# Row sums of squares as two fp32r products, the second half a unit later

## The reference

```python
def rmsnorm(x, g):
    xf = x.astype(jnp.float32)
    y = xf * lax.rsqrt(jnp.mean(xf * xf, axis=-1, keepdims=True) + EPS)
    return (y * g).astype(x.dtype)

for l in range(DEPTH):                      # first_block
    if l < N_A:  x = x + short_conv_mixer(rmsnorm(x, attn_norm[l]), ...)
    else:        # k, v, c from rmsnorm(x, kv_norm); q, gate from rmsnorm(x, attn_norm[l])
        c = jnp.cumsum(jax.nn.log_sigmoid(f_logit), axis=1)
        ...
        x = x + o @ b_w_out[j]
    x = x + conv_ffn(rmsnorm(x, ffn_norm[l]), ...)
# second_block
h = _rms_norm(x, norm_mix_g[l]);  proj = h @ w_in[l]
...
x = x + merged @ w_out[l]
x = x + (jax.nn.silu(ff_gate) * ff_up) @ w_ffn_out[l]
```

## Time and profile before

| what | value |
|---|---|
| median of 3 runs | 2110.87 us (2110.78 to 2111.08) |
| the profiled execution, its own time | 2110.74 us |
| its span in the profile | 2108.9 us |
| PE busy | 2081.9 us, 99% |
| POOL busy | 1498.7 us, 71% |
| DVE busy | 927.7 us, 44% |
| ACT busy | 475.0 us, 23% |
| granted clock of TensorE | 1.00 |
| share of PE in the chain that ended last | 93% |

### The profile page before, as it was taken

The page is one execution under the profiler, slowest core; times in us unless marked ns, Lnnn a source line. Parts: engine busy times, 40 slices in busy tenths (PEclk is TensorE's granted clock), DMA queues, the critical chain, the costliest instruction groups (busy, mean ns, idle before and its releaser), DMA issues.

```text
span 2108.9 us, 29655 instructions
## 1 busy us (share of the span) xinstructions
PE 2081.9 (99%) x10652; PEld 1755.5 (83%) x10652; DVE 927.7 (44%) x1406; ACT 475.0 (23%) x977; POOL 1498.7 (71%) x1607
## 2 busy tenths in 40 slices
PE   7999999999999999999999999999999999999999
PEld 6888888888798887888888889989877888888887
DVE  6655655521445555655541166436643243222100
ACT  2002111100345554211100053231343112111000
POOL 6788888868854456888877766546545787777675
PEclk9999999999999999999999999999999999999999
DMA  4333333223432232333323333223322333333232
GB/s 153 94 110 103 99 99 91 86 84 101 116 92 81 81 91 75 99 91 99 99 72 96 102 87 85 65 71 81 83 68 70 90 100 93 96 99 99 73 93 85
DMA packets 368007, 192.65 MB, mean 91 GB/s; under 512 B 8640, under 2 KB 364320, under 8 KB 367920
## 3 DMA queue, kind: packets, MB, share of 16 engines
q1 hardware_dynamic: 364672, 186.28, 30.8%
q10 hardware_dynamic: 3248, 5.20, 0.8%
HBM read 189.32 MB, written 2.13 MB: 91 GB/s over the span
## 4 chain that ended last, share of the span: by engine, by line
PE 93%; DVE 4%; ACT 3%; issue 1%; ACTq 0%; DMA 0%; DVEq 0%
PE PS L519 22%; PE PS L521 22%; PE PS L520 22%; PE PS L801 2%; PE PS L803 2%; PE PS L802 2%; PE PS L817 2%; PE PS L819 2%; PE PS L818 2%; PE PS L684 2%; PE PS L686 2%; PE PS L685 2%; PE PS L999 1%; PE PS L1018 1%; PE PS L629 1%
## 5 line engine op out<-in xcount | busy, mean ns | idle before, releaser
L502 POOL TENSOR_TENSOR RING<-RAW,RING 128x512 fp32r<-128x512 f32 x704 | 966.9, 1373 | 58.7
L499 POOL TENSOR_SCALAR RING<-RAW 128x512 fp32r<-128x512 f32 x704 | 514.0, 730 | 376.2 <-PE PS L686 99.1
L519 PE MATMUL PS<-XH,RING 128*128 128x512 f32 x1336 | 522.2, 391 | 3.7 <-DVE XT L2232 2.5
L521 PE MATMUL PS<-XH,RING 128*128 128x512 f32 x1336 | 519.8, 389 | 0.0
L520 PE MATMUL PS<-XL,RING 128*128 128x512 f32 x1336 | 519.8, 389 | 0.0
L519 PEld LDWEIGHTS PS<-XH,RING 128*128 128x128 f32 x1336 | 250.8, 188 | 58.1 <-DVE XT L2232 2.7
L520 PEld LDWEIGHTS PS<-XL,RING 128*128 128x128 f32 x1336 | 250.8, 188 | 52.9 <-issue 1.2
L521 PEld LDWEIGHTS PS<-XH,RING 128*128 128x128 f32 x1336 | 250.8, 188 | 52.1
L519 PE MATMUL PS<-HH,RING 128*128 128x512 f32 x528 | 205.6, 389 | 0.0
L521 PE MATMUL PS<-HH,RING 128*128 128x512 f32 x528 | 205.4, 389 | 0.0
L520 PE MATMUL PS<-HL,RING 128*128 128x512 f32 x528 | 205.4, 389 | 0.0
(11 more groups left out here) (307 smaller groups left out, 3278.9 us busy)
## 6 DMA issues: line engine op xcount, KB each, us to landing
RAW<-in_ffn_w_up SPq DMA_DIRECT2D x88, 512.0 KB, 3.7
RAW<-in_w_in SPq DMA_DIRECT2D x52, 512.0 KB, 3.6
RAW<-in_w_ffn_in SPq DMA_DIRECT2D x44, 512.0 KB, 3.7
RAW<-in_ffn_w_down SPq DMA_DIRECT2D x32, 512.0 KB, 3.8
RAW<-in_a_w_in SPq DMA_DIRECT2D x24, 512.0 KB, 3.6
RAW<-in_b_w_qg SPq DMA_DIRECT2D x16, 512.0 KB, 3.7
RAW<-in_w_kvf SPq DMA_DIRECT2D x16, 512.0 KB, 3.8
RAW<-in_w_ffn_out SPq DMA_DIRECT2D x16, 512.0 KB, 3.7
```

The costliest lines, as they stand in the source:

```text
L499: hi = pool.tensor_scalar(WH[s][:, k0_:k1, :], RAW[s][:, k0_:k1, :], 1.0, 1.0, ALU.mult, ALU.mult)
L502: lo = pool.tensor_tensor(WL[s][:, k0_:k1, :], RAW[s][:, k0_:k1, :], WH[s][:, k0_:k1, :].bitcast(F32), ALU.subtract)
L519: pe.matmul(o, WH[s][:, k, :], xh[:, k0 + k, :], start=first and k == 0, stop=False)
L521: mm = pe.matmul(o, WL[s][:, k, :], xh[:, k0 + k, :], start=False, stop=last and k == nk - 1)
```

## The change

- The fp32 product of a row sum becomes two fp32r products into the same bank: ONE by ACCH, then ONE by ACCL. ACCH is the accumulated squares W[1] rounded to fp32r, ACCL the remainder. DVE makes both at the end of `residual`, behind the last XL, and signals `acc_split` after each; PE waits for the first and for the second. ACCH lies over W[3], ACCL over W[2].
- The place: in `ffn` and in `attention` the sum now stands in the middle of the second unit, 12 products later; in `gla` behind `gla_dense(0, 1)`, also 12 products later.
- ONE is filled by a memset in place of a copy of the constants.

```diff
+        ACCH = at("ACCH", [P, S], F32R, W_at[3])
+        ACCL = at("ACCL", [P, S], F32R, W_at[2])
...
             def row_sums(n):
 
-                pe.wait_ge(sem("acc"), tiles(n) + KT)
-                pe.matmul(PS[:, 7, :], ONE[:, :], W[1][:, 0:S], start=True, stop=True).then_inc(sem("nsum"), 1)
+                one = ONE[:, :].bitcast(F32R)
+                pe.wait_ge(sem("acc_split"), 2 * n + 1)
+                pe.matmul(PS[:, 7, :], one, ACCH[:, :], start=True, stop=False)
+                pe.wait_ge(sem("acc_split"), 2 * n + 2)
+                pe.matmul(PS[:, 7, :], one, ACCL[:, :], start=False, stop=True).then_inc(sem("nsum"), 1)
...
+                            if isinstance(i, int) and i == 0 and q == 0 and k == 1:
+                                half_unit(pu, 1, 0, 1, XH, XL)
+                                row_sums(n)
+                                half_unit(pu, 1, 1, 1, XH, XL)
+                                continue
                             unit(pu, i, 2 * q + k, 2 * q + k, XH, XL,
                                  ready=(sem("xld"), 1, scaled(n)) if isinstance(i, int) and i == 0 and q == k == 0 else None)
-                            if isinstance(i, int) and i == 0 and q == k == 0:
-                                row_sums(n)
...
                 unit(p, 0, 0, 0, XH, XL, ready=(sem("xld"), 1, scaled(1)))
+                half_unit(p, 1, 0, 1, XH, XL)
                 row_sums(1)
-                unit(p, 0, 1, 1, XH, XL)
+                half_unit(p, 1, 1, 1, XH, XL)
                 unit(p, 0, 2, 2, XH, XL)
...
                 gla_dense(0, 0)
+                gla_dense(0, 1)
                 row_sums(3)
-                for n in range(1, 3):
-                    gla_dense(0, n)
+                gla_dense(0, 2)
                 pe.wait_ge(sem("narrow"), 4)
...
                 loop(dve, iters, body, steps)
+                if gains:
+                    dve.wait_ge(sem("acc"), tiles(n) + KT)
+                    dve.tensor_copy(ACCH[:, :], W[1][:, 0:S]).then_inc(sem("acc_split"), 1)
+                    dve.wait_ge(sem("acc_split"), 2 * ORDER[n] + 1)
+                    dve.tensor_tensor(ACCL[:, :], W[1][:, 0:S], ACCH[:, :].bitcast(F32), ALU.subtract).then_inc(
+                        sem("acc_split"), 1)
...
-            for to, c in ((IDF, C_ID), (ONE, C_ONE), (MCAUSAL, C_CAUSAL), (MUPPER, C_UPPER)):
+            dve.memset(ONE[:, :], 1.0)
+            for to, c in ((IDF, C_ID), (MCAUSAL, C_CAUSAL), (MUPPER, C_UPPER)):
```

## The result

| | before | changed |
|---|---|---|
| median of 20 runs each | 2110.74 us | 2114.86 us |
| lowest to highest | 2110.16 to 2111.08 | 2112.27 to 2118.77 |
| ratio of the medians | | 1.0021 [1.0014, 1.0027] |
| the profiled execution, its own time | 2110.74 | 2113.73 |
| its span | 2108.9 | 2111.9 |

The median lies 4.1 us higher and the spread grew from 0.9 to 6.5 us. Of the twenty runs one has a granted clock of 1.000, and it is the fastest; the others have 0.999 (2113.5 to 2114.1) and 0.998 or 0.997 (2114.6 to 2118.8). Only one of the twenty has a trace. Lines of the changed kernel stand a little lower in its file: L535 and L537 are the two passes, L810 a half unit's product, L692 the token piece's, L937 the transposes, L1645 the norm's first step, L1679 and L1681 the split, L1706 an eviction of the feed-forward.

The account below looks back on a forecast made before the run. PE, busy 2081.9 of 2108.9 us, was taken as the bound. Feed-forward -1.22, n = 3 +2.10 and n = 1 +2.32 gave +3.2 on 2110.74, so 2113.9 us; range 2111.7 to 2116.5.

Parts of the forecast that it names:

- The product: At each of five row sums, two fp32r passes of 0.455 us replace 0.86 on PE, saving 0.405 each, 2.03 in all.
- rival (d): At the row sums, an fp32r pass with ONE costs 0.86 like the fp32 product: +9.5 us, 2120.3; 2%.
- The split: DVE's copy and subtraction behind each residual's last XL take 1.12 to 2.90 us, hidden by 12 products, costing nothing.
- Feed-forward: Behind sums n = 0, 2, 4: seven us of room hide the 2.32 us delay; change 3 x -0.405 = -1.22.
- n = 3: Gated linear attention: with 0.37 us of room, PE waits for LRT and the transposes of W[0] start 2.10 us later.
- n = 1: Attention: the whole chain to KN moves by 2.32 us, making PE's wait about 4.3; +2.3, between 0.9 and 3.3.
- My bound for this stretch: Attention chain, n = 1: up to 1.4 us could come back from held-up DVE steps, L1627 and four X2L.
- Rival (b): The pause of about 4.3 us at n = 1 lets the clock fall to half: some 3 us more, 2116.8; 8%.
- 1.00 throughout: Over the whole span, the granted clock was forecast to stay at full level, so no pause costs more than its length.
- (a): Every chain behind the later sums has room, so only PE's saving stays: -2.03 us, 2108.7; 7% with the half cases.
- (c): The n = 1 chain stretches by over 1.2 us, from the store meeting transfers and DVE steps beside POOL: 2115.2 to 2116.5; 10%.

Follow-up runs that it names:

- product_only: Changed kernel with all row sums back at their old places, the split and the two fp32r passes kept; median 2110.89 us.
- n3_cover: Changed kernel with gla_dense(0, 3) moved ahead of the wait for LRT and the transposes at n = 3; median 2112.18 us.
- late_with_room: n3_cover with DVE's attention order of bias_early, the n = 1 sum staying at its later place; median 2108.61 us.
- bias_early: both_undone with gates 0 and 1 and the forget gate's bias moved ahead of the last two X2L on DVE; median 2107.19 us.
- n1_old: Changed kernel with only the row sum of n = 1 back in its old place, still two fp32r products; median 2112.09 us.
- both_undone: Changed kernel with the n = 1 sum at its old place and gla_dense(0, 3) ahead of the wait at n = 3; median 2109.23 us.
- n1_later3: Changed kernel with the row sum of n = 1 three products (0.68 us) later; median 2114.09 us.
- place_only: Kernel before with the row sums at the later places and ONE's memset, still one fp32 product, no split; median 2115.13 us.
- n1_later: Changed kernel with the row sum of n = 1 a further 12 products (2.72 us) later, behind the whole second unit; median 2113.87 us.
- n3_filled: n1_old with nine products that nobody reads ahead of the wait for LRT at n = 3; median 2111.93 us.
- n1_earlier3: Changed kernel with the row sum of n = 1 three products (0.68 us) earlier; median 2111.94 us.
- n1_filled: Changed kernel with 14 products that nobody reads ahead of the first piece of part 1 at n = 1; median 2113.70 us.

## Why the prediction was right where it was, and wrong where it was not

**The sum.** Forecast +3.2, 2113.9. The profiled execution came out at 2113.73, +3.0, but not by the steps of the forecast: the restart behind KN came 0.8 earlier than I said, a wait of 0.8 at 660 went away, and a fall of the clock brought 1.5 that were not in the forecast. That these three nearly cancel is luck. The median has 1.1 more, most likely by further falls. The lower bound was added up wrongly too: 2113.9 - 1.4 - 0.1 is 2112.4, not 2112.3.

**The product: right.** 0.24 and 0.23 in the chain, and steps of -0.37 to -0.43 at every sum where -0.405 was said. fp32r with ones as the stationary tile streams like the others; rival (d) is out.

**The split: right.** 1.51 + 0.69 = 2.20, inside 1.12 to 2.90, and no wait for it. product_only shows what it costs uncovered: 0.4 to 1.3 a site, where I had written up to 2.9.

**Feed-forward: right.** The eviction that began at 204.72 begins at 208.13; I said 207.04, so there was 1.1 more in between. It is hidden by the room of seven us all the same: the only steps there are the products'.

**n = 3: right in mechanism and size.** The transposes move from 1225.77 to 1229.13. The site's two steps, -0.39 and +2.38, are +2.0, where +2.10 was said. n3_cover takes the wait away, and the further half unit costs 0.9 us later on: cheaper, not free.

**n = 1: mechanism right, size wrong.** The step that failed here is that the whole chain from the sum to KN moves as one. I moved it by 2.32, giving a pause of 4.3. It is 3.52, and the restart is 1.55 later instead of 2.32 (from -0.43 to +1.12). Walk down the chain with both kernels. The norm's first step on DVE begins at 563.04, +1.91 by the clock of the trace; that is 2.32 less the 0.4 by which PE is early there. The forget step is still +2.05. The changed kernel, DVE, start us, us, what:

```profile
563.04 0.69 DVE L1645 TENSOR_SCALAR W<-PS 128x512 f32<-128x512 f32 x1 [2.01 <-PE PS L537]
...
582.34 0.69 DVE L1838 SCALAR_TENSOR_TENSOR W<-W,W 128x512 f32<-128x512 f32 x1 [3.53 <-ACT W L1328]
583.06 1.23 DVE L1840 TENSOR_TENSOR_SCAN W<-W,W 128x512 f32<-128x512 f32 x1
```

The same two steps in the kernel before:

```profile
580.29 1.11 DVE L1823 SCALAR_TENSOR_TENSOR W<-W,W 128x512 f32<-128x512 f32 x1 [3.39 <-ACT W L1319]
581.44 1.52 DVE L1825 TENSOR_TENSOR_SCAN W<-W,W 128x512 f32<-128x512 f32 x1
```

They take 0.71 less now, since POOL has no step from 582.00 on in the changed kernel, and one of 2.08 us from 581.97 before. So the store is issued +1.34. Then the store itself: before issued at 584.17 and used at 586.99; now, ACT's queue in the changed kernel:

```profile
585.51 0.33 ACTq L1333 DMA_DIRECT2D cums<-W  x1
...
587.12 0.83 ACTq L1299 DMA_DIRECT2D W<-cums  x2
```

1.6 us in place of 2.8: +0.13 is left. The windows of 583 to 585 and 585 to 587, before and then after, columns as above, show what it met (DMA share and GB/s are the last two columns):

```profile
583.00:585.00 2.00, 2.00 (x19) 2.00 (x18) 1.13 (x2) 1.41 (x3) 1.05 (x1) 1.00 0.00 0
585.00:587.00 2.00, 2.00 (x19) 2.00 (x19) 0.00 (x0) 1.10 (x1) 0.00 (x0) 1.00 0.84 223
```

```profile
583.00:585.00 2.00, 2.00 (x19) 2.00 (x19) 1.97 (x4) 0.70 (x2) 0.00 (x0) 1.00 0.87 224
585.00:587.00 2.00, 2.00 (x19) 2.00 (x18) 0.47 (x1) 1.98 (x3) 0.00 (x0) 1.00 0.20 55
```

Before, the 32 KB store was issued just ahead of a 512 KB weight slice: the slice's packets run from 585.10 to 587.70, the store's from 585.77 to 586.66, in the midst of them. In the changed kernel the slice is over at 585.58 and the store's packets run from 586.35 to 586.74. In late_with_room it is issued at 583.35 and used at 586.17, 2.8 again; in bias_early 1.6; in n1_old and both_undone, issued at 584.54 and 584.55, 1.9 and 2.0, used at 586.4 and 586.5. The store's first packet comes 1.6 to 1.7 behind its issue where a slice begins in between (before, late_with_room), and 0.8 to 0.9 where the slice ran already or none ran (changed, n1_old, both_undone, bias_early). So for issues from 583.4 to 585.5 the end moves by less than one us. That the weight slice is the cause is inferred from where the transfers stand in these six traces; no run moved the slice alone. The prediction had the direction wrong: it said that meeting a slice might cost 1.0 more, and did not see that the 2.80 already held it.

Last, one us comes back. In the changed kernel:

```profile
590.34 1.20 DVE L1635 SCALAR_TENSOR_TENSOR TINY<-TINY 128x8 f32<-128x8 f32 x1 [0.76 <-ACT TINY L1184]
...
590.25 1.26 POOL L504 TENSOR_TENSOR RING<-RAW,RING 128x512 fp32r<-128x512 f32 x1
```

A step of 8 columns takes 1.20 where it takes 0.17 alone, and ends at 591.53, 0.02 behind POOL's subtraction at 591.51. With it KN is +1.12. In n1_later3 the second step of the pair takes 1.22 and ends at 594.39, POOL's at 594.37. Its pause is 0.6 shorter than the changed kernel's, as nothing but KN follows that step.

The same collision explains why seven kernels have the same pause of 1.79, wherever their sum stands (n1_old, both_undone, place_only, product_only, n1_later, n3_filled, n1_earlier3). POOL begins a split 0.09 us behind PE's last product, which released it: first a step of 0.62, then one of 1.27. In all seven DVE's first small step falls beside the 0.62 and ends 0.01 to 0.02 behind it; KN, and with it PE, follow at a fixed distance. In n1_old:

```profile
589.63 0.47 DVE L1635 SCALAR_TENSOR_TENSOR TINY<-TINY 128x8 f32<-128x8 f32 x1 [0.76 <-ACT TINY L1184]
...
589.47 0.62 POOL L501 TENSOR_SCALAR RING<-RAW 128x512 fp32r<-128x512 f32 x1 [7.23 <-PE PS L694]
```

So a chain that comes up to some 0.3 us earlier or later ends at the same time, and one that misses the short step meets the long one and is held for 1.2, as in the changed kernel. In place_only the store goes out behind its slice and the small step takes 0.30 beside the short POOL step, so its restart is only +0.2.

The same collision is behind the wait at 660 that vanished. Before, DVE and POOL there:

```profile
655.72 1.19 DVE L1758 SCALAR_TENSOR_TENSOR TINY<-TINY 128x8 f32<-128x8 f32 x1
...
657.66 1.19 DVE L1626 SCALAR_TENSOR_TENSOR TINY<-TINY 128x8 f32<-128x8 f32 x1 [0.76 <-ACT TINY L1175]
```

```profile
655.60 1.28 POOL L502 TENSOR_TENSOR RING<-RAW,RING 128x512 fp32r<-128x512 f32 x1
...
657.55 1.27 POOL L502 TENSOR_TENSOR RING<-RAW,RING 128x512 fp32r<-128x512 f32 x1
```

Both end 0.02 behind POOL's. In the changed kernel they take 0.19 and 0.62. The page "SBUF — State Buffer" of the Trainium skill, section "Who interferes with whom", says that a DVE instruction with two SBUF inputs contends with a GpSimd instruction that reads SBUF, and that the ports they share are locked by one of them at a time. The ends above agree. My bound for this stretch named held-up steps of 512 columns, and not that the small ones can lose as much.

**Rival (b), given 8%: its mechanism happened.** I wrote that it decides only if a pause of four us is enough. In the profiled execution 3.5 was, in those of other kernels 1.8 and 2.2, and nineteen of twenty runs of the changed kernel lie at least 1.2 above the one with full clock. Its price, some 3 us, was too high for this execution. A fall costs 1.48 us here (the shift goes from 1.12 to 2.60), 1.4 to 1.6 in both_undone, place_only, n1_earlier3 and n1_later3, and 2.4 in n3_cover, where the clock was low for twice as long. The groups of n1_old, 1.5 apart, fit one and two falls. The page "TensorE: Matmul & The Clock Gate" of the Trainium skill, section "Why this matters for your kernels", warns against long gaps between bursts, since the clock then falls to half. The trace agrees, with 0.50 behind a pause of 3.5 us. The prediction weighed it by the earlier trace rows alone, where a pause of 2.45 was followed by full clock. Counting the runs that lie 1 us or more above the group of their kernel's lowest:

| pauses of the profiled execution | kernel | runs 1 us or more above |
|---|---|---|
| none | bias_early | 0 of 11 |
| 1.6 | before; late_with_room | 3 of 99; 0 of 11 |
| 1.8 | both_undone; product_only | 4 of 11; 3 of 11 |
| 1.8 (n = 3 filled) | n3_filled | 6 of 11 |
| 2.2 | n1_filled | 6 of 11 |
| 1.8 and 2.2 | n1_old; n1_earlier3 | 8 of 11; 7 of 10 |
| 1.8, 2.0 and 2.2 | n1_later | 5 of 11 |
| 2.9 and 2.2 | n1_later3 | 7 of 10 |
| 3.5 and 2.2 | changed | 19 of 20 |

n3_cover (3.5) and place_only (1.8 and 2.2) are not in it. By their shifts they should lie near 2110.7 and 2113.5 without a fall, and their lowest runs are 2111.99 and 2115.01, so neither seems to have a run without one. The counts are read from times: only one run of each kernel has a trace. They tell no pause at all from one of 3.5, but with 10 or 11 runs they do not rank the pauses between. Nor need every fall be at one of the two pauses: n1_later3 and n3_cover had one near the start too, at 23 and at 15 us. A clock of 0.999 alone shows no loss either: in product_only it comes from the last 2.5 us of the span, where PE had no product left.

I forecast 1.00 throughout, and this was the main step that failed. Without falls the sum of the shifts is +1.5, and the run at full clock, 2112.27, is 1.5 above 2110.74. So by that run the forecast of +3.2 was twice the loss at full clock, the median's other 2.6 us go with the clock, and that 2114.86 came near 2113.9 is in good part luck. What makes one execution fall and another not, at the same pause, is open, and so is what makes the slowest runs of the changed kernel 6.5 us slower than its fastest, since none of them has a trace.

**Rivals (a) and (c).** Neither chain had room for 2.3 us, so (a) is out, but n = 1 had 0.8 of it. (c) expected held-up steps beside POOL and a store in traffic; the first came (1.0), the second had been there before.

## What to carry to other kernels

Before you move a step later, walk the chain behind it to the engine that bounds, site by site, and put cover in front of the wait before you take it away: here the saving of 2.0 us on PE was real, and the chains behind two of the five sums gave more than that back. Read a transfer or a step that is longer than its like as a collision that may end when it is moved, and the fast ones as collisions that may begin. On an engine that is busy 99% price a new pause, even one of two us, as its length and, some of the time, a fall of the clock on top.

## What the runs showed of the hardware

- The granted clock fell to half after pauses of TensorE of 1.8, 2.2, 2.9 and 3.5 us in the middle of dense work, for some 3 us or more. It began while the engine still stood (n3_cover) or up to 1.5 us behind the restart (n1_later3; 0.9 in the changed kernel). A fall cost 1.4 to 1.6 us, and 2.4 where the clock was low for some 7 us. Other executions had the same pauses of 1.8 and 2.2 us and kept the full clock (n1_old).
- A VectorE step of 8 columns with two SBUF inputs took 1.2 us beside a GpSimd subtraction of two tiles, 0.30 to 0.60 beside a GpSimd step of 0.62 that it ended with, and 0.17 to 0.19 alone.
- A 32 KB store to DRAM took 1.6 us, and 2.8 where a 512 KB load began between its issue and its first packet.
- VectorE's cast of 128x512 from f32 to fp32r took 1.51 us, at n = 0 and at n = 3 (product_only), the plain copy of that size 0.43 at its shortest.
- Two fp32r passes of 512 columns with ones as the stationary tile cost TensorE 0.23 each; the fp32 product 0.86.
